# Moving the end of a decoder-layer kernel into the programs of its expert stage

## The reference

```
for each expert e, for each token t routed to it (1024 tokens, 8 experts each):
    acc[t] += weight[t, e] * ((silu(h[t] @ w1[e]) * (h[t] @ w3[e])) @ w2[e])
acc += shared expert
out = x2 + g2 * rmsnorm(acc, norm_post_ffn)
```

## Time and profile before

| | us |
|---|---|
| median of 3 runs (lowest, highest) | 2011.83 (2010.6, 2017.6) |
| span of the profiled execution | 2006.3 |
| median of the runs less that span | 5.5 |
| PE busy, share of the span | 1802.1, 90% |
| DVE busy | 1379.2, 69% |
| ACT busy | 1118.5, 56% |
| POOL busy | 459.1, 23% |

### The profile page before, as it was taken

How to read it: one execution, slowest core, us unless ns; L and a number is a source line. 1 busy time by engine, 2 the same in 40 slices (tenths; PEclk the granted TensorE clock), 3 DMA queues, 4 the chain that set the end, 5 groups by cost and what they waited for, 6 DMA issues and landing times. The chain is left out here.

```text
span 2006.3 us, 38325 instructions
## 1 busy us (share of the span) xinstructions
PE 1802.1 (90%) x10165; PEld 1321.2 (66%) x10166; DVE 1379.2 (69%) x2601; ACT 1118.5 (56%) x2164; POOL 459.1 (23%) x360
## 2 busy tenths in 40 slices
PE   3999999776799779998699999999999999999992
PEld 3778887454688544444477777777676777777771
DVE  6598731785588343534488888878787878887885
ACT  3411221676566221312477777777777777777774
POOL 0012000000122103225033323333233332333320
PEclk9999999997899788998899999999999999999996
DMA  9268501301100472311679978899889998799955
GB/s 348 74 192 239 162 37 33 125 17 58 42 8 11 137 299 65 86 43 45 216 221 309 274 232 270 248 303 327 237 239 303 308 306 278 216 300 320 309 160 179
DMA packets 167949, 380.05 MB, mean 189 GB/s; under 512 B 31045, under 2 KB 43678, under 8 KB 164780
## 3 DMA queue, kind: packets, MB, share of 16 engines
q1 hardware_dynamic: 132844, 288.38, 41.1%
q0 software_dynamic: 35024, 90.60, 18.6%
HBM read 333.26 MB, written 82.13 MB: 207 GB/s over the span
## 5 line engine op out<-in xcount | busy, mean ns | idle before, releaser
L2195 DVE TENSOR_TENSOR w_low<-w_experts,w_high 128x1024 fp32r<-128x1024 f32 x392 | 461.8, 1220 | 87.4 <-issue 62.9
L2144 ACT CAST w_high<-w_experts 128x1024 fp32r x394 | 394.0, 1049 | 86.8 <-issue 82.4
L2126 POOL DMA_INDIRECT acc<-y_rows,scatter_idx x96 | 187.7, 1955 | 636.1 <-DMA acc<-y_rows,scatter_idx 319.6
L2257 PE MATMUL ps_h<-w_high,xT_high 128*128 128x512 f32 x776 | 315.6, 407 | 9.0 <-DVE xT_low L2210 9.0
L2257 PE MATMUL ps_h<-w_high,xT_low 128*128 128x512 f32 x776 | 307.8, 397 | 0.0
L2257 PE MATMUL ps_h<-w_low,xT_high 128*128 128x512 f32 x776 | 307.3, 396 | 0.0
L2279 PE MATMUL ps_y<-w_experts,actT 128*128 x384 | 185.0, 604 | 14.1 <-issue 12.0
L2257 PEld LDWEIGHTS ps_h<-w_high,xT_high 128*128 128x128 f32 x776 | 147.3, 190 | 40.2 <-issue 7.3
L2257 PEld LDWEIGHTS ps_h<-w_high,xT_low 128*128 128x128 f32 x776 | 146.1, 188 | 35.2
L2257 PEld LDWEIGHTS ps_h<-w_low,xT_high 128*128 128x128 f32 x776 | 146.6, 189 | 31.1
L2109 POOL DMA_INDIRECT gathered<-h,idx x96 | 136.0, 1417 | 46.0 <-issue 45.7
(11 more groups left out here) (414 smaller groups left out, 3358.8 us busy)
## 6 DMA issues: line engine op xcount, KB each, us to landing
w_experts<-in_exp_w SPq DMA_DIRECT2D x512, 256.0 KB
w_experts<-in_exp_w SPq DMA_DIRECT2D x128, 512.0 KB
qT<-in_w_ada POOLq DMA_DIRECT2D x16, 1024.0 KB, 8.1
w_raw<-in_w_in SPq DMA_DIRECT2D x24, 512.0 KB, 7.0
w_ada<-in_w_ada SPq DMA_DIRECT2D x8, 1024.0 KB, 11.9
p_mixed<-mixed SPq DMA_DIRECT2D x8, 512.0 KB, 8.0
w_out<-in_w_out SPq DMA_DIRECT2D x1, 4096.0 KB, 12.5
x_kept<-x SPq DMA_DIRECT2D x8, 512.0 KB
```

The costliest lines, as they stand in the source:

```text
L2126: pool.indirect_dma_start(dr["acc"], bass.IndirectOffsetOnAxis(ap=sidx[j][:], axis=0), y[j % 2][:], None, bounds_check=S - 1, oob_is_err=F ...
L2144: act.copy(w13_s[par][0][:, which, k], w13[:, bass.ds(w, 1), which, k].squeeze(1)).then_inc(w_high, 1)
L2195: dve.tensor_tensor(w13_s[par][1][:, which, k], w13[:, bass.ds(w, 1), which, k].squeeze(1), w13_s[par][0][:, which, k], ALU.subtract).then ...
L2257: q = pe.matmul(ps_h[:].rearrange("p (a n) -> p a n", a=2), xT[a][:, k, :], w13_s[par][z][:, :, k, :], start=(k == 0 and m == 0), stop=(k ...
```

## The change

The block `finish` is removed, and its instructions are appended to the programs of the five engines in `experts`. There is then no barrier between the two.

- SP: behind its last load it waits for `y_out >= 16 * nb`, which is the landing of the scatter of the last real block, and issues the 8 loads of `acc`. The stores follow as before.
- The 8 tiles of `acc` go to `acc_at`: the 6 tile-sized pieces of slot 0, one of slot 1's `w2` and one of slot 2's; the statistics go into slot 2's other one. The products and the squares go to `spare_at`, over `w13_high` and `w13_low`.
- ACT: behind its loop come the table load, a wait until DVE has done all its reads of `w13_high` (`w_low`), and the same 8 times three instructions, each tile waiting for its landing.
- DVE: behind its loop it waits for the copy of the last block's result (`y_ready`, behind which PE has read `w13_high` and `w13_low`) and for `post2`, and then does the same 16 instructions.
- POOL and PE: unchanged. POOL still waits for all scatters of the last turn, then ends.
- `c_slot_step`: padding blocks now find the slot of expert 63 (slot 3) in the table, where before they found slot 0.

```diff
-def experts(nc, io, dr, keep):
+def experts(nc, io, dr, keep, out):
...
+        post, x2 = keep["post2"], [keep["x2"][t // 4][:, t % 4, :] for t in range(NT)]
+        acc_tile = [nc.alloc_sbuf_tensor_at(f"acc_tile{t}", [P, D], F32, offset=keep["acc_at"][t]) for t in range(NT)]
+        acc_post = [nc.alloc_sbuf_tensor_at(f"acc_post{t}", [P, D], F32, offset=keep["spare_at"] + t * D * 4) for t in range(NT)]
+        squares = [nc.alloc_sbuf_tensor_at(f"acc_squares{n}", [P, D], F32, offset=keep["spare_at"] + (NT + n) * D * 4) for n in range(2)]
...
             sp.dma_start(keep["post2"][:], dr["rows"][:, 5 * D:6 * D].partition_broadcast(P)).then_inc(keep["post_in"], 16)
+            sp.wait_ge(y_out, n_blocks(sp) * 16)
+            for t in range(NT):
+                sp.dma_start(acc_tile[t][:], dr["acc"][t * P:(t + 1) * P, :]).then_inc(acc_in[t], 16)
+            for t in range(NT):
+                sp.wait_ge(sums, t + 1)
+                sp.dma_start(out[0][t * P:(t + 1) * P, :], x2[t]).then_inc(outs, 16)
+            sp.wait_ge(outs, 16 * NT)
...
+            load_exp_and_ln(nc, act)
+            f_after = Steps(act, f_step)
+            act.wait_ge(w_low, (nb + 3) // 4 * 16 + 8)
+            for t in range(NT):
+                act.wait_ge(acc_in[t], 16)
+                f_after.then(act.activation(squares[t % 2][:], acc_tile[t][:], ACT.Square, accum_out=f_st[:, t, 0:1]))
...
+            dve.wait_ge(y_ready, (nb + 3) // 4 * 4 + 1)
+            dve.wait_ge(keep["post_in"], 16)
+
+            def times_post(t):
+                dve.wait_ge(acc_in[t], 16)
+                dve.tensor_tensor(acc_post[t][:], acc_tile[t][:], post[:], ALU.mult).then_inc(posted, 1)
...
-def finish(nc, io, dr, keep, out):
...
-        "c_slot_step": f(np.broadcast_to([[(e + 1) % SLOTS - e % SLOTS] for e in range(E)], (E, P))),
+        "c_slot_step": f(np.broadcast_to([[min(e + 1, E - 1) % SLOTS - e % SLOTS] for e in range(E)], (E, P))),
...
+            keep["acc_at"] = [slots_at + n * D * 4 for n in (0, 1, 2, 3, 4, 5, 11, 16, 17)]
+            keep["spare_at"] = (nc.sbuf_base + 31) // 32 * 32
```

More of the change, by code:

```diff
@@ L2059, in experts @@
         TURNS = (BLOCKS + 3) // 4
+        post, x2 = keep["post2"], [keep["x2"][t // 4][:, t % 4, :] for t in range(NT)]
+        acc_tile = [nc.alloc_sbuf_tensor_at(f"acc_tile{t}", [P, D], F32, offset=keep["acc_at"][t]) for t in range(NT)]
+        acc_post = [nc.alloc_sbuf_tensor_at(f"acc_post{t}", [P, D], F32, offset=keep["spare_at"] + t * D * 4) for t in range(NT)]
+        squares = [nc.alloc_sbuf_tensor_at(f"acc_squares{n}", [P, D], F32, offset=keep["spare_at"] + (NT + n) * D * 4) for n in range(2)]
+        f_st = nc.alloc_sbuf_tensor_at("f_stats", [P, NT, 3], F32, offset=keep["acc_at"][NT])
+        f_step, acc_in = sem("f_act_step"), [sem(f"acc_in{t}") for t in range(NT)]
+        f_rstd, posted, sums, outs = sem("f_rstd"), sem("f_posted"), sem("f_sums"), sem("f_out")
         block = ctx.enter_context(nc.Block())
@@ L2180, in _ @@
                         act.copy(y[j % 2][:, BANK:], ps_y[1][:]).then_inc(y_ready, 1)
+            load_exp_and_ln(nc, act)
[4 more added lines that the diff above has]
+                f_after.then(act.activation(squares[t % 2][:], acc_tile[t][:], ACT.Square, accum_out=f_st[:, t, 0:1]))
+                f_after.then(act.activation(f_st[:, t, 1:2], f_st[:, t, 0:1], ACT.Ln, scale=1.0 / D, bias=keep["eps"][:, 0:1]))
+                act.activation(f_st[:, t, 2:3], f_st[:, t, 1:2], ACT.Exp, scale=-0.5).then_inc(f_rstd, 1)
         @block.vector
@@ L2239, in _ @@
                     step.restart()
+            dve.wait_ge(y_ready, (nb + 3) // 4 * 4 + 1)
[3 more added lines that the diff above has]
+                dve.tensor_tensor(acc_post[t][:], acc_tile[t][:], post[:], ALU.mult).then_inc(posted, 1)
+            times_post(0)
+            for t in range(NT):
+                if t + 1 < NT:
+                    times_post(t + 1)
+                dve.wait_ge(keep["x2_in"][t // 4], 64)
+                dve.wait_ge(posted, t + 1)
+                dve.wait_ge(f_rstd, t + 1)
+                dve.scalar_tensor_tensor(x2[t], acc_post[t][:], f_st[:, t, 2:3], x2[t], ALU.mult, ALU.add).then_inc(sums, 1)
         @block.tensor
@@ L2450, in build @@
             keep["x2"] = [nc.alloc_sbuf_tensor_at(f"x2_kept{half}", [P, 4, D], F32, offset=slots_at + (1 + half) * 3 * KC * F * 4) for half in range(2)]
-            experts(nc, io, dr, keep)
-            finish(nc, io, dr, keep, out)
+            keep["acc_at"] = [slots_at + n * D * 4 for n in (0, 1, 2, 3, 4, 5, 11, 16, 17)]
+            keep["spare_at"] = (nc.sbuf_base + 31) // 32 * 32
+            experts(nc, io, dr, keep, out)
 DUMP = ["rows", "mixed", "ymix", "x2", "h2", "acc", "out_x"]
```

## The result

| | before | changed |
|---|---|---|
| median, 10 runs each on one chip, us | 2013.77 | 2000.8 |
| the same without one run of 6229 us | 2011.83 | 2000.8 |
| lowest of these | 2004.57 | 1994.86 |
| span of the profiled execution | 2006.3 | 2003.7 |
| from the last copy of `y_rows` to the end of the span | 36.4 | 26.6 |

The ratio of the times is 0.9946 with a 95% interval of 0.993 to 0.9963: the changed kernel is faster by 0.54% (0.37% to 0.70%), some 10.9 us (7.4 to 14.1). One of the ten runs of before took 6229 us; the ratio leaves it out, and so the figure to compare with 2000.8 is 2011.83, the median of the other nine. The forecast was 2002.0 us, 9.8 less.

What follows compares the result with a forecast made beforehand. The end was taken as a chain: POOL's drain, barrier, first load (3.7 us), DVE's pass (18.8), store (3.1). First sum at 1976.85 instead of 1986.68 gives 2011.8 - 9.8 = 2002.0 us, range 1999.5 to 2005.5.

Steps and rivals of the forecast that it cites:

- The load of acc: Behind SP's wait for the last real scatter: first load issued at 1967.5, landing 1971.2; loads 13.0 us earlier.
- Rival 1: SP's wait met only by the turn's last scatter, about 1973.4; loads 7.1 us earlier, total 2004.7; chance 0.04.
- one of its signs of being wrong: New trace: prediction wrong if the time in front of 1967 moves by more than 1 us.
- Rival 2: ACT's table load has a tail: 2002.7 us by rows, 2003.4 with the skill's 1380 ns drain; chance 0.04.
- The empty turns: End of expert loop: 8 empty turns, 0.63 us each on ACT, 0.74 on DVE, keep both until 1973.7.
- Rival 3: Empty turns aren't on the path at the loop's end; first sum 13.0 us earlier, total 1998.8; chance 0.03.
- Rival 4: DVE's two-input operations wait for POOL's drain in the last pass; 4.0 us less, total 2007.8; chance 0.03.
- POOL's drain now runs from 1974.8: Behind the expert loop: POOL's 5.46 us drain runs to 1980.3 beside DVE's pass, 16 us ahead of the last barrier.
- Rival 5: Expert loop starts to fetch code, 1.3 us in each of 24 real turns; +21.6, total 2033.4; chance 0.02.
- needs no fetch: Way from loop to last pass: code already in the engines' buffers, no instruction-queue packet from 1040 to 1980.
- The sum: Whole kernel: first sum 9.8 us earlier, span 1996.5; median 2011.8 - 9.8 = 2002.0 us; likeliest case 0.84.
- the line of 0.5%: Whole kernel: 10.1 us is distinguishable from no change; faster by over 0.5%: 0.48, within 0.5%: 0.50.

Runs made afterwards that it cites:

- the first experiment: Changed kernel, but SP waits for all scatters of the last turn (96), not the 95 real blocks'; from last copy of `y_rows` to span end 29.75 us.
- counted loops: Changed kernel with POOL, ACT, DVE and PE loops counted to real turns instead of 32; ratio 0.9941 against the kernel before.
- the second comparison: Changed kernel timed again without an edit, against the kernel before on the same chip: median 1998.04 against 2008.49 us, ratio 0.995.

## Why the prediction was right

**The load of acc.** Forecast at C - 2.4, measured at C - 2.6; tile 0 3.8 us later. That the last scatter is padding was read from 0.00 MB, and the first experiment confirms it: with a wait for that scatter the loads come 6.5 us later relative to C. Rival 1 is excluded.

**In front of C.** Counted from C, each link that sets the time came as the prediction has it. Counted from the start of the span nothing did, and by the letter one of its signs of being wrong came up: the time in front of C moved by 7.3 us, not by less than 1, and the span was 2003.7, not 1996.5. Over the ten profiles C lies anywhere from 1962.8 to 1978.0, with 1974.8 in the second one of the changed kernel, so a single profile can't bear that sign. It should have been put on the stretches from C on.

**ACT.** Table load forecast 3.84 behind C, measured 3.81. The gap between table load and square, for which I had bounds of 0 and 0.73 and took 0.05, is 0.02 (1982.25 to 1982.27). Rival 2 falls. The drain of some 1380 ns that the Trainium skill names ("ScalarE: Activation LUTs", What ACT_TABLE_LOAD costs) doesn't stand behind the load here, and with counted loops, where the load begins 0.02 behind C, it doesn't stand in front of it either. One slip had no effect: tile 0 was said to land 2.5 us before ACT wants it, which is counted to the table load; to the first square it is 3.9 (C + 1.2 to C + 5.1).

**The empty turns.** Rival 3 falls by the counted loops, where ACT leaves at C. Their price on the path was expected at 3.3 and measured at 2.8 and 3.3 in the two profiles.

**DVE.** Products from C + 4.0 (forecast 4.1), held 0.55 (0.5), first sum at C + 6.95 in place of C + 16.8: 9.8 earlier, as forecast. DVE's durations are unchanged, 16.47 us from the start of the first sum to the end of the last (forecast 16.46). Rival 4, in which POOL's drain holds DVE, falls: between 1985.7 and 1991.1, beside the drain, DVE's operations take 1.22 and 1.28 as elsewhere. But the mechanism that I argued away with the loop's scatters is real when POOL computes. What I cited against it, 392 operations beside POOL's DMA work, says nothing of POOL's own arithmetic.

**Store and end.** 3.1 us again. The cover of POOL's drain was there, but thinner than I wrote: I had the drain end at C + 10.4, 16 us before the last barrier; it ended at C + 14.0, 12 before it. The step "POOL's drain now runs from 1974.8" is the one that failed, since I moved 4 MB of loads in front of a scatter on the same 16 DMA engines and didn't ask what they do to it: the scatter landed at C + 8.4 to C + 8.9 and not at C + 3.6. It cost nothing only because nothing waits for POOL there.

**Slower.** Rival 5 needed 0.41 us a turn; the page of the changed kernel shows as many packets on the instruction queues as before (49 and 32), and the expert loop took 995.3 us against 996.3. One of these packets lies behind C in both kernels, so "needs no fetch" says too much about the pass; it moved with the pass, and no wait goes with it.

**The sum.** The difference, 9.8, is what the tail gave (36.39 - 26.57) and lies within the measured 7.4 to 14.1. The absolute number had luck in its base. It came from the median of three runs, of a kernel whose runs go from 2004.57 to 2017.6; the nine runs without the outlier have the very same median, 2011.83, and so the forecast is only 1.2 too high. The 5.5 us that I put around the span aren't around it. The changed kernel's runs lie 1.8 above their own spans (2005.54 and 2003.7 for the profiled one), so the profiled execution of before should have lasted some 2008.1 us (estimate from that 1.8), and the other 3.7 are the distance of that one execution from the median; in which stages it was quicker isn't shown. Whether the gain is above or below the line of 0.5%, on which the chances were nearly even, the runs leave open: 0.54% with 0.37% to 0.70% here, 0.50% with 0.32% to 0.68% in the second comparison.

## What to carry to other kernels

A barrier between two stages costs what its slowest member still does when all useful work is over; look at the sequencers' rows, where a drain of 5.5 us and eight turns of an empty loop stand that no busy share tells of. Price the removal of a barrier together with what is moved across it, since with the barrier in place the early loads brought nothing, and the two together brought more than the barrier by itself. And when whole runs scatter by more than the gain, cut the trace at the last instruction that the change can't touch, and compare the stretch behind it.

## What was not expected of the hardware

- A scatter of 144 packets without data landed in 2.7 us with the DMA engines free and in 7.3 us behind 4 MB of loads from another queue.
- A 128 by 1024 float32 product takes 1.22 us on DVE and some 2.2 on POOL. Where they meet, the later one waits for the earlier to end: 3.36 to 3.38 us for DVE's, 2.6 to 3.4 for POOL's.
- POOL's DRAIN at the end of the expert block took 5456 ns in all eight profiles without a product on POOL, whatever moved beside it. With POOL's last product still running when it began it took 8.2 and 7.9, and both times it ended 5.5 behind that product. What it waits for isn't shown.
- An empty turn of a loop costs ACT's sequencer 0.63 us, DVE's 0.74 and POOL's 0.45, though it only compares and jumps.
